# A decoder step on one core: the key/value stage rebuilt around pairs of tiles and four split slots

## The chip, the cores and the metric

The kernel runs on one core of a Trainium2 chip. The metric is the device time of one execution in microseconds. Three executions of the kernel before took 1482.45, 1484.24 and 1484.52 us; the median is 1484.24.

## What is computed

One inference step of a one-layer decoder, for a prompt of 1024 tokens and 8 sample tokens, model width 1024, all in float32. The outputs are the tokens, the caches, and for the prompt the keys and values of a memory of 256 tokens. What touches this change is the first half of it:

```python
def memory_kv(mem, g, w_k, w_v):          # mem: 256 tokens x 1024
    m = rms_norm(mem, g)
    return m @ w_k, m @ w_v               # keys and values, both are outputs

h = rms_norm(x, norm_mix_g)               # x: 1032 tokens x 1024
proj = h @ w_in                           # 2576 columns, 21 tiles of 128 with padding
...
x = x + token_mix(...)                    # convolution and gated linear attention, w_out
x = x + cross_attn(rms_norm(x), mk, mv)   # w_q, w_o
x = x + square(relu(rms_norm(x) @ w_up)) @ w_down
y = rms_norm(x, final_g)
```

## The kernel before

**Tiles.** Activations lie with features on the 128 partitions and the 1032 tokens (T) along the free side, in blocks of 344 (CB). Weights come as tiles of 1024 x 128 (512 KB, 8 slices k of 128 x 128), numbered t. Tiles 0 to 15 are w_xk and w_xv (stage "kv", T_IN = 16), then 21 tiles of w_in, and so on up to the last.

**Split products.** Each product is made in float32r as three: high x high, high x low, low x high. So each weight tile is split: ACT copies it, rounded, to the high half (w_high, L676), POOL subtracts that from the raw tile in two halves of four slices and gets the low half (lo, L602). PE then multiplies (tile_product, L1166, in the kv stage 8 slices x 3 products = 24 matmuls of 256 columns, m_op being the split memory). The raw tile comes by a DMA that SP issues (load_w, L453). In the kv stage there are four raw slots (w_raw, w_more; tile t in slot t % 4) but two split slots in w_split: w_high(t) waits until tile t-2 is multiplied (tile_done), and load_w(t) until lo(t-4) is done. An engine takes its own instructions in the order in which they are written.

**The kv stage.** m_raw (the memory) comes in two DMAs, par (gains) in one. ACT issues the four loads of x (load_x, L691), walpha and conv_cache in its own queue. ACT makes the eight high parts of memory (L705) with the gain in them, DVE the low ones (L1736). ACT squares the memory (L707), DVE adds the squares over the slices (L1744), PE sums them over the partitions with a matrix of ones (sums, L1185), behind tile 0, and ACT makes the root by Ln and Exp (L711, L713): m_rstd. DVE evacuates each tile from the bank set it lies in, PS[t % 2], with m_rstd as factor (kv_evac, L1760). Keys go out from m_out; values are transposed by PE in pairs (mv_turn, L1199), read by ACT (mv_read, L738), and go out. SP's stores of mk and mv stand in its order between the loads, with waits for kv_evac or mv_read ahead of them (L476, L479).

**The norm of x in the same stage.** ACT squares the eight parts of x (square_x, L718 and L722), DVE adds them into acc in SBUF (add_square, L1769), PE sums over the partitions behind tile 8, into the two small banks M (L1185, three products, the third of which waits for a bank), ACT makes 1/rms by Ln and Exp (norm, L683 and L687) into rstd in SBUF, DVE multiplies x by it and the gain (x_scale, L1772), ACT rounds to a_op high (x_high, L732), DVE subtracts (x_low, L1735). The first input tile (first_in_tile, L1281) waits for x_low(k) slice by slice and writes all three banks of PS[0]; the other input tiles (in_block, L1267) follow block by block. From the second input tile on DVE works on the convolution's taps (L1806), which accumulate in PS[1].

In the code ORDER, PLACE and SLOTS set what PE does between tiles; SP, POOL, ACT, PE and DVE each have a block of their own in build(). The three functions of the norm and the order of ACT's and DVE's work in the stage are written out by hand:

```python
for t in range(2, 11):                                   # ACT
    w_high(t, t % 2)
    for k in {3: (0, 1), 4: (2, 3), 6: (4, 5), 7: (6, 7)}.get(t, ()):
        square_x(k)
norm(1, 1)
...
for n_kv in range(9):                                    # DVE
    kv_evac(n_kv)
    for k in {2: (0, 1), 3: (2, 3), 5: (4, 5), 6: (6, 7)}.get(n_kv, ()):
        add_square(k)
```

## Time and profile before

| | us |
|---|---|
| median of three executions | 1484.24 |
| the profiled execution | 1484.24 |
| its span in the trace | 1482.2 |
| PE busy in the span | 1446.8 (98%) |
| DVE / ACT / POOL busy | 611.1 / 461.8 / 387.0 |
| first product of PE (kv stage) | 11.05 |
| first input tile | 87.49 |
| granted clock, mean of the span | 0.994 |

The page cuts the span into 40 slices of 37 us; a digit is the busy share in tenths:

```profile
PE   5799999999999999999999999999999999999998
PEld 5789999999899999979999999999999999999997
DVE  3659999998553355633321200121011111012114
ACT  5532243436733333413232200132012221022324
POOL 4754222111722211102222222222222222222220
PEclk9999999999999999999999999999999999999999
```

PE is TensorE's matmuls, PEld its weight loads, DVE VectorE, ACT ScalarE, POOL GpSimd; PEclk is the clock granted to TensorE, where 1.00 is 2.4 GHz and 0.50 is 1.2 GHz. Times in all rows are microseconds from the span's start unless marked ns.

### The profile page before, as it was taken

To read this page: it belongs to the slowest core of one execution; us is meant where nothing else is said; L and a number is where in the kernel's file an instruction comes from. 1 tells how busy PE (TensorE), PEld (TensorE's weight loads), DVE (VectorE), ACT (ScalarE), POOL (GpSimd) and SP (SyncE) were. 2 spreads that over 40 slices of the span, in tenths; PEclk is the share of its full clock that TensorE was granted. 3 is DMA by queue.
4 is the path that set the end of the run, shared out by engine and by line. 5 is a ranking of instruction groups with operands and counts; after the bars stand their busy time and mean duration, and the time that the engine had idled before them with its cause. 6 is when DMAs were issued, how large, how long until landed. Compare 5 with 4: busy or idle time off the path is not lost.

```text
span 1482.2 us, 22520 instructions
## 1 busy us (share of the span) xinstructions
PE 1446.8 (98%) x9501; PEld 1414.9 (95%) x9501; DVE 611.1 (41%) x693; ACT 461.8 (31%) x622; POOL 387.0 (26%) x298
## 2 busy tenths in 40 slices
PE   5799999999999999999999999999999999999998
PEld 5789999999899999979999999999999999999997
DVE  3659999998553355633321200121011111012114
ACT  5532243436733333413232200132012221022324
POOL 4754222111722211102222222222222222222220
PEclk9999999999999999999999999999999999999999
DMA  7421151102252511392111111111111111111113
GB/s 283 151 74 50 51 51 47 40 29 56 92 186 101 185 58 35 104 372 75 43 43 57 43 47 52 43 42 57 42 42 42 42 57 42 56 37 48 43 42 115
DMA packets 47357, 114.06 MB, mean 77 GB/s; under 512 B 7720, under 2 KB 23352, under 8 KB 45888
## 3 DMA queue, kind: packets, MB, share of 16 engines
q1 hardware_dynamic: 46544, 108.41, 23.7%
q10 hardware_dynamic: 752, 4.75, 0.8%
q8 instruction: 48, 0.79, 0.2%
q14 instruction: 13, 0.11, 0.0%
HBM read 100.85 MB, written 12.30 MB: 76 GB/s over the span
## 4 chain that ended last, share of the span: by engine, by line
PE 93%; DVE 4%; ACT 1%; POOL 1%; issue 1%; DMA 0%; ACTq 0%; SPq 0%; DVEq 0%
PE ps L1166 59%; PE ps L1267 14%; PE ps L1539 5%; PE m L1237 2%; PE ps L1573 2%; PE ps L1671 1%; PE ps L1492 1%; PE m L1452 1%; POOL w_split L602 1%; PE ps L1281 1%; DVE ps L1806 1%; PE ps L1552 1%; PE m L1367 1%; PE m L1516 1%; PE ps L1483 1%
## 5 line engine op out<-in xcount | busy, mean ns | idle before, releaser
L602 POOL TENSOR_TENSOR w_split<-w_raw,w_split 128x512 fp32r<-128x512 f32 x234 | 326.4, 1416 | 1044.7 <-ACT w_split L676 1044.5
L1166 PE MATMUL ps<-a_op,w_split 128*128 128x344 f32 x3168 | 499.4, 319 | 0.0
L1166 PEld LDWEIGHTS ps<-a_op,w_split 128*128 128x128 f32 x3168 | 497.8, 188 | 0.5 <-issue 0.5
L1166 PE MATMUL ps<-b_op,w_split 128*128 128x344 f32 x2304 | 362.6, 319 | 0.0
L1166 PEld LDWEIGHTS ps<-b_op,w_split 128*128 128x128 f32 x2304 | 361.7, 188 | 0.2
L1267 PE MATMUL ps<-a_op,w_split 128*128 128x344 f32 x1440 | 233.2, 321 | 0.0
L1267 PEld LDWEIGHTS ps<-a_op,w_split 128*128 128x128 f32 x1440 | 226.5, 188 | 1.7 <-issue 1.4
L676 ACT ACTIVATE w_split<-w_raw 128x1024 fp32r<-128x1024 f32 x117 | 122.9, 1051 | 258.5 <-PE ps L1166 252.4
L1806 DVE SCALAR_TENSOR_TENSOR ps<-conv_in,par,ps 128x1024 f32<-128x1024 f32 x116 | 149.7, 1291 | 3.6
L2192 DVE SCALAR_TENSOR_TENSOR tmp<-ps,rstd 128x1032 f32<-128x1032 f32 x32 | 39.5, 1233 | 215.1 <-PE ps L1166 203.2
L2202 DVE TENSOR_TENSOR x_res<-x_res,ps 128x1032 f32 x24 | 29.5, 1229 | 230.8 <-PE ps L1166 230.8
L1097 ACT ACTIVATE tmp<-tmp 128x1032 f32<-128x1032 f32 x32 | 34.1, 1067 | 259.1 <-DVE tmp L2192 259.1
L1539 PE MATMUL ps<-b_op,w_split 128*128 128x344 f32 x504 | 83.3, 322 | 0.0
L1539 PEld LDWEIGHTS ps<-b_op,w_split 128*128 128x128 f32 x504 | 79.8, 188 | 0.6
L2014 DVE TENSOR_TENSOR x_res<-x_res,ps 128x1032 f32<-128x1032 f32 x22 | 27.0, 1228 | 129.2 <-PE ps L1166 124.8
L1166 PE MATMUL ps<-m_op,w_split 128*128 128x256 f32 x384 | 57.9, 313 | 21.8 <-POOL w_split L602 21.8
L1166 PEld LDWEIGHTS ps<-m_op,w_split 128*128 128x128 f32 x384 | 54.3, 218 | 24.8 <-issue 17.8
L2197 DVE TENSOR_TENSOR a_op<-tmp,a_op 128x1032 f32 x32 | 39.5, 1234 | 80.8 <-ACT a_op L1100 80.8
L979 ACT ACTIVATE b_op<-x_res,par 128x1032 fp32r<-128x1032 f32 x16 | 18.6, 1160 | 101.9 <-DVE x_res L2014 101.9
L1100 ACT ACTIVATE a_op<-tmp 128x1032 f32 x32 | 34.2, 1067 | 4.3
L1736 DVE SCALAR_TENSOR_TENSOR b_op<-x_res,par,b_op 128x1032 fp32r<-128x1032 f32 x16 | 22.8, 1422 | 19.7 <-ACT b_op L979 19.7
L722 ACT ACTIVATE tmp<-x_res 128x1032 f32<-128x1032 f32 x19 | 20.1, 1056 | 33.1 <-DVE x_res L2014 33.0
(245 smaller groups left out, 1070.6 us busy)
## 6 DMA issues: line engine op xcount, KB each, us to landing
w_raw<-in_wt SPq DMA_DIRECT2D x117, 512.0 KB, 3.5
cache_b<-in_cache_v SPq DMA_DIRECT2D x8, 1024.0 KB, 12.2
x_in<-in_x ACTq DMA_DIRECT2D x4, 1032.0 KB, 10.7
x_spill<-x_res SPq DMA_DIRECT2D x8, 516.0 KB, 2.6
w_more<-in_wt SPq DMA_DIRECT2D x8, 512.0 KB, 4.1
cache_a<-in_cache_k SPq DMA_DIRECT2D x2, 2048.0 KB, 11.2
cache_b<-in_cache_k SPq DMA_DIRECT2D x2, 2048.0 KB, 11.8
x_res<-in_x SPq DMA_DIRECT2D x1, 3096.0 KB, 11.1
```

The lines of the kernel that those rows point to most:

```text
L602: gp.tensor_tensor(w_split[:, slot, 1, part, :], src, w_split[:, slot, 0, part, :].bitcast(F32), ALU.subtract).then_inc(w_low_done, 1)
L676: act.activation(w_split[:, slot, 0, :, :], src, ACT.Copy).then_inc(w_high_done, 1)
L1097: act.activation(tmp[:, j, :], tmp[:, j, :], ACT.Square).then_inc(scalar_step, 1)
L1100: act.activation(dst, tmp[:, j, :], ACT.Copy).then_inc(hidden_high, 1)
L1166: last = pe.matmul(ps[:, c0 // CB, 0:w], w_split[:, slot, wp, k, :], src[:, k, xp, c0:c0 + w], start=(k == 0 and j == 0), stop=(k == KT - ...
L1237: last = pe.matmul(bank[:, j * C:(j + 1) * C], k_t[:, pair, NS + C * c:NS + C * (c + 1)], qz[pair][:, C * c:C * (c + 1)], start=True, stop ...
L1267: last = pe.matmul(PS[0][:, b, 0:CB], w_split[:, p % 2, wp, k, :], a_op[:, k, xp, b * CB:(b + 1) * CB], start=(k == 0 and j == 0), stop=(k ...
L1539: last = pe.matmul(PS[0][:, b, 0:CB], w_split[:, t % 2, wp, k, :], b_op[:, k, xp, b * CB:(b + 1) * CB], start=(k == 0 and j == 0), stop=(k ...
L1573: last = pe.matmul(PS[m][:, b, 0:CB], w_split[:, t % 2, wp, k, :], a_op[:, k, xp, b * CB:(b + 1) * CB], start=(k == 0 and j == 0), stop=(k ...
L1806: link(dve.scalar_tensor_tensor(out=conv_acc, in0=src, scalar=t_, in1=conv_acc, op0=ALU.mult, op1=ALU.add))
L2192: dve.scalar_tensor_tensor(out=cols(tmp[:, j, :]), in0=pcols(bank_of(T_FF + j)), scalar=0.0, in1=cols(rstd[:, :]), op0=ALU.max, op1=ALU.mu ...
L2197: dve.tensor_tensor(dst, tmp[:, j, :], hi, ALU.subtract).then_inc(hidden_low, 1)
```

## The change

Four split slots: two more (w_split_more) lie in a_op's parts 6 and 7, which are not yet in use; kv tile t takes split slot t % 4, w_high(t) waits for tile t-4, and x_high(6), x_high(7) wait for tiles 14 and 15 to be done. Two kv tiles share one bank of PS[0], and three banks take turns (kv_pair); DVE evacuates a pair at once (128x512), so 8 evacuations stand for 16. PS[1] is free for x: the running sum of squares, the sums over the partitions and 1/rms lie there; only the last add goes to acc in SBUF. Memory's 1/rms is Sqrt on ACT and a reciprocal on DVE; a small Sqrt ahead of everything and a small Ln behind the root are new. The memory's sums stand behind tile 2. All loads go through SP's queue, par and w0 first, the parts of x behind tiles 3, 5, 6 and 7. The stores of mk and mv and the third pair of mv transposes change their place. ACT's and DVE's order is written anew.

```diff
 for _g in range(4):
-    SLOTS.setdefault((PLACE["kv", 9 + 2 * _g] + 1, LAST_BLOCK), []).append(("mv", _g))
+    SLOTS.setdefault((PLACE["kv", 9 + 2 * _g] + (1, 1, 2, 1)[_g], LAST_BLOCK), []).append(("mv", _g))
 for _j in range(2 * NB):
...
 assert o_sm + DC * 4 <= o1 + SPLIT + KT * T * 4
+w_split_more = [at(f"w_split_more{i}", (KT - 2 + i) * 2 * T * 4, [P, 2, KT, P], F32R) for i in range(2)]
 w_more = at("w_more", o_u, [P, 2, KT, P])
...
+def split(t, slot):
+    return w_split_more[slot] if isinstance(t, int) and t < T_IN and t % 4 >= 2 else w_split[:, slot]
+def kv_pair(g):
+    return PS[0][:, g % NB, :].rearrange("p (a n) -> p a n", a=2)
 a_products = tmp[:, :, :].rearrange("p a n -> p (a n)")
...
 def _(sp):
-    sp.dma_start(m_raw[:, 0:4, :], a["mem"][:, 0:4, :]).then_inc(m_part[0], 16)
     sp.dma_start(par[:, :], a["par"]).then_inc(params_loaded, 16)
...
+    def load_x(i):
+        sp.dma_start(x_in[:, 2 * i:2 * i + 2, :], a["x"][:, 2 * i:2 * i + 2, :]).then_inc(x_part[i], 16)
     load_w(0, 0, False)
-    sp.dma_start(m_raw[:, 4:8, :], a["mem"][:, 4:8, :]).then_inc(m_part[1], 16)
+    for i in range(2):
+        sp.dma_start(m_raw[:, 4 * i:4 * i + 4, :], a["mem"][:, 4 * i:4 * i + 4, :]).then_inc(m_part[i], 16)
     for t in range(1, 4):
         load_w(t, t % 2, False)
+    load_x(0)
     for t in range(4, T_XO + 3):
         load_w(t, t % 2)
+        if 5 <= t < 8:
+            load_x(t - 4)
+        if t == 9:
+            sp.dma_start(walpha[:, :], a["w_alpha"]).then_inc(w_alpha_loaded, 16)
+            sp.dma_start(conv_smp[:, :, :, :], a["conv_cache"]).then_inc(conv_cache_loaded, 16)
         for q in range(4):
-            if t == PLACE["kv", 2 * q + 1] + 5:
+            if t == 2 * q + 8:
                 sp.wait_ge(ps_free, PLACE["kv", 2 * q + 1] + 1)
                 sp.dma_start(o["mk"][:, 2 * q:2 * q + 2, :], m_out[:, q % 2, :, :]).then_inc(mem_kv_stored[q % 2], 16)
-            if t == PLACE["kv", 9 + 2 * q] + (6, 6, 7, 7)[q]:
+            if t == (16, 17, 19, 20)[q]:
                 wait_read(sp, ("mv", q))
...
             src = raw(t)[:, part, :] if isinstance(t, int) else w_raw[:, slot, part, :]
-            gp.tensor_tensor(w_split[:, slot, 1, part, :], src,
-                             w_split[:, slot, 0, part, :].bitcast(F32), ALU.subtract).then_inc(w_low_done, 1)
+            gp.tensor_tensor(split(t, slot)[:, 1, part, :], src,
+                             split(t, slot)[:, 0, part, :].bitcast(F32), ALU.subtract).then_inc(w_low_done, 1)
...
             act.wait_ge(w_loaded[slot], (count - 4) * 16 + 16)
-        if not isinstance(t, int) or t >= 2:
-            act.wait_ge(tile_done, t - 1)
+        if not isinstance(t, int) or t >= 4:
+            act.wait_ge(tile_done, t - 3 if isinstance(t, int) and t < T_IN + 2 else t - 1)
         src = raw(t) if isinstance(t, int) else w_raw[:, slot, :, :]
-        act.activation(w_split[:, slot, 0, :, :], src, ACT.Copy).then_inc(w_high_done, 1)
+        act.activation(split(t, slot)[:, 0, :, :], src, ACT.Copy).then_inc(w_high_done, 1)
...
-    def load_x(i):
-        act.dma_start(x_in[:, 2 * i:2 * i + 2, :], a["x"][:, 2 * i:2 * i + 2, :]).then_inc(x_part[i], 16)
+    act.wait_ge(eps_ready, 1)
+    act.activation(small[:, 129:130], small[:, 128:129], ACT.Sqrt)
+    w_high(0, 0)
     act.wait_ge(params_loaded, 16)
-    load_x(0)
     for k in range(KT):
...
             act.wait_ge(m_part[k // 4], 16)
-        if k == 4:
-            w_high(0, 0)
-            for i in range(1, 4):
-                load_x(i)
-            act.dma_start(walpha[:, :], a["w_alpha"]).then_inc(w_alpha_loaded, 16)
-            act.dma_start(conv_smp[:, :, :, :], a["conv_cache"]).then_inc(conv_cache_loaded, 16)
         act.activation(m_op[:, k, 0, :], m_raw[:, k, :], ACT.Copy,
                        scale=par[:, G_MEM + k:G_MEM + k + 1]).then_inc(operand_high, 1)
+    w_high(1, 1)
+    w_high(2, 0)
     act.activation(msq[:, :, :], m_raw[:, :, :], ACT.Square).then_inc(square_done, 1)
-    w_high(1, 1)
-    act.wait_ge(eps_ready, 1)
-    act.wait_ge(sums_ready, 1)
-    act.activation(m_rstd[:, :], M[0][:, 0:MEM], ACT.Ln, bias=small[:, 128:129], scale=1.0 / D).then_inc(sums_read, 1)
-    act.wait_ge(sums_read, 1)
-    act.activation(m_rstd[:, :], m_rstd[:, :], ACT.Exp, scale=-0.5).then_inc(rstd_ready, 1)
+    w_high(3, 1)
+    def mem_root():
+        act.wait_ge(sums_ready, 1)
+        act.activation(m_rstd[:, :], M[0][:, 0:MEM], ACT.Sqrt, bias=small[:, 128:129], scale=1.0 / D).then_inc(sums_read, 1)
+        act.activation(small[:, 131:132], small[:, 128:129], ACT.Ln)
...
             act.wait_ge(x_part[k // 2], 16)
-        square(x_in[:, k, :], None, k, 1)
+        if k == 0:
+            act.activation(pcols(1), cols(x_in[:, 0, :]), ACT.Square).then_inc(square_done, 1)
+        else:
+            square(x_in[:, k, :], None, k, 1)
+    def norm_x():
+        act.wait_ge(sums_ready, 1 + NB)
+        act.activation(cols(rstd[:, :]), pcols(1), ACT.Ln, bias=small[:, 128:129], scale=1.0 / D).then_inc(sums_read, NB)
+        act.wait_ge(sums_read, 1 + NB)
+        act.activation(pcols(1), cols(rstd[:, :]), ACT.Exp, scale=-0.5).then_inc(rstd_ready, 1)
...
         act.wait_ge(x_normed, k + 1)
+        if k >= KT - 2:
+            act.wait_ge(tile_done, T_IN - KT + 1 + k)
         act.activation(a_op[:, k, 0, :], x_in[:, k, :], ACT.Copy).then_inc(operand_high, 1)
...
-    for t in range(2, 11):
+    square_x(0)
+    square_x(1)
+    w_high(4, 0)
+    w_high(5, 1)
+    mem_root()
+    square_x(2)
+    square_x(3)
+    w_high(6, 0)
+    square_x(4)
+    square_x(5)
+    w_high(7, 1)
+    square_x(6)
+    w_high(8, 0)
+    square_x(7)
+    for t in range(9, 13):
         w_high(t, t % 2)
-        for k in {3: (0, 1), 4: (2, 3), 6: (4, 5), 7: (6, 7)}.get(t, ()):
-            square_x(k)
-    norm(1, 1)
-    for k in range(KT):
-        x_high(k)
-        if k >= 1:
-            w_high(10 + k, k % 2)
-        if k in (2, 4, 6):
-            mv_read((k - 2) // 2)
+    norm_x()
+    w_high(13, 1)
+    x_high(0)
+    x_high(1)
+    w_high(14, 0)
+    x_high(2)
+    x_high(3)
+    mv_read(0)
+    w_high(15, 1)
+    x_high(4)
+    x_high(5)
+    w_high(16, 0)
+    mv_read(1)
+    w_high(17, 1)
+    x_high(6)
+    x_high(7)
+    mv_read(2)
...
+    def kv_product(n):
+        if n % 2 == 0 and n >= 2 * NB:
+            pe.wait_ge(ps_free, n - 2 * NB + 2)
+        bank = kv_pair(n // 2)[:, n % 2, :]
+        w_ = split(n, n % 2)
+        for k in range(KT):
+            if k % (KT // 2) == 0:
+                pe.wait_ge(w_low_done, n * 2 + 1 + k // (KT // 2))
+            if n == 0:
+                pe.wait_ge(operand_low, k + 1)
+            for j, (wp, xp) in enumerate(((0, 0), (0, 1), (1, 0))):
+                last = pe.matmul(bank, w_[:, wp, k, :], m_op[:, k, xp, :], start=(n % 2 == 0 and k == 0 and j == 0),
+                                 stop=(n % 2 == 1 and k == KT - 1 and j == 2))
+        last.then_inc(tile_done, 1)
+    def x_sums():
+        pe.wait_ge(squares_summed, 1 + KT)
+        for b in range(NB):
+            pe.matmul(PS[1][:, b, 0:CB], ones[:, :], acc[:, b * CB:(b + 1) * CB], start=True, stop=True).then_inc(sums_ready, 1)
     def first_in_tile():
...
-        pe.wait_ge(ps_free, T_IN - 1)
+        pe.wait_ge(ps_free, T_IN)
         for k in range(KT):
...
                 if name[1] == 0:
-                    pe.wait_ge(sums_read, 4)
+                    pe.wait_ge(sums_read, 1)
                 mv_turn(name[1])
...
     for n_kv in range(T_IN):
-        tile_product(n_kv, n_kv % 2, m_op, [(0, MEM)], wait_lo(0) if n_kv == 0 else no_wait)
-        if n_kv == 0:
+        kv_product(n_kv)
+        if n_kv == 2:
             sums(1, 0, MEM)
         if n_kv == 8:
-            sums(9, 1)
+            x_sums()
         between(n_kv, LAST_BLOCK)
...
-    def kv_evac(n):
-        p = PLACE["kv", n]
-        dve.wait_ge(tile_done, p + 1)
-        if n == 0:
+    def kv_evac(g):
+        dve.wait_ge(tile_done, 2 * g + 2)
+        if g == 0:
             dve.wait_ge(rstd_ready, 1)
-        g = n // 2
-        if n < 8:
-            dst = m_out[:, g % 2, n % 2, :]
-            if g >= 2 and n % 2 == 0:
+        if g < 4:
+            dst = m_out[:, g % 2, :, :]
+            if g >= 2:
                 dve.wait_ge(mem_kv_stored[g % 2], 16)
         else:
-            dst = mvt[:, g % 2, n % 2, :]
-            if g >= 6 and n % 2 == 0:
+            dst = mvt[:, g % 2, :, :]
+            if g >= 6:
                 wait_full(dve, ("mv", g - 6))
-        dve.tensor_tensor(dst, PS[p % 2][:, 0, 0:MEM], m_rstd[:, :], ALU.mult).then_inc(ps_free, 1)
+        dve.tensor_tensor(dst, kv_pair(g), m_rstd[:, :].unsqueeze(1).broadcast_to([P, 2, MEM]), ALU.mult).then_inc(ps_free, 2)
...
             dve.engine_nop().then_inc(squares_summed, 1)
-        else:
-            dve.wait_ge(squares_summed, 1 + k)
-            dve.tensor_tensor(acc[:, :], acc[:, :], tmp[:, k % 2, :], ALU.add).then_inc(squares_summed, 1)
+            return
+        dve.wait_ge(squares_summed, 1 + k)
+        if k == KT - 1:
+            dve.wait_ge(sums_ready, 1)
+        dst = pcols(1) if k < KT - 1 else cols(acc[:, :])
+        dve.tensor_tensor(dst, pcols(1), cols(tmp[:, k % 2, :]), ALU.add).then_inc(squares_summed, 1)
...
     def x_scale(k):
-        dve.scalar_tensor_tensor(out=x_in[:, k, :], in0=x_in[:, k, :], scalar=par[:, G_MIX + k:G_MIX + k + 1],
-                                 in1=rstd[:, :], op0=ALU.mult, op1=ALU.mult).then_inc(x_normed, 1)
+        dve.scalar_tensor_tensor(out=cols(x_in[:, k, :]), in0=cols(x_in[:, k, :]), scalar=par[:, G_MIX + k:G_MIX + k + 1],
+                                 in1=pcols(1), op0=ALU.mult, op1=ALU.mult).then_inc(x_normed, 1)
...
-    for n_kv in range(9):
-        kv_evac(n_kv)
-        for k in {2: (0, 1), 3: (2, 3), 5: (4, 5), 6: (6, 7)}.get(n_kv, ()):
-            add_square(k)
+    add_square(0)
+    add_square(1)
+    dve.wait_ge(sums_read, 1)
+    dve.reciprocal(m_rstd[:, :], m_rstd[:, :]).then_inc(rstd_ready, 1)
+    add_square(2)
+    kv_evac(0)
+    add_square(3)
+    kv_evac(1)
+    add_square(4)
+    add_square(5)
+    kv_evac(2)
+    add_square(6)
+    add_square(7)
+    kv_evac(3)
     dve.wait_ge(rstd_ready, 2)
...
     x_scale(1)
-    for k in range(7):
-        kv_evac(9 + k)
+    kv_evac(4)
+    x_scale(2)
+    x_scale(3)
+    x_scale(4)
+    kv_evac(5)
+    x_scale(5)
+    x_scale(6)
+    x_scale(7)
+    kv_evac(6)
+    for k in range(4):
         x_low(k)
-        if k + 2 < KT:
-            x_scale(k + 2)
-    x_low(KT - 1)
+    kv_evac(7)
+    for k in range(4, KT):
+        x_low(k)
+    dve.wait_ge(x_normed, KT)
     n_taps = 0
     conv_acc = PS[1][:, 0:2, :]
...
```

## Rows read from the trace of the kernel before

**Rows 1.** Windows: stretch, length, busy us (instructions) per engine, clock, DMA share, GB/s.
```profile
99.47:340.00 240.53, 240.53 (x1576) 237.26 (x1576) 220.47 (x200) 83.93 (x134) 63.53 (x63) 1.00 0.22 47
```

**Rows 2.** Timeline of PE: start, length, instructions, [idle before, releaser].
```profile
11.05 5.46 PE L1166 MATMUL ps<-m_op,w_split 128*128 128x256 f32 x24 [11.05 <-POOL w_split L602]
...
24.94 11.64 PE L1166 MATMUL ps<-m_op,w_split 128*128 128x256 f32 x72 [3.17 <-POOL w_split L602]
...
52.15 1.32 PE L1185 MATMUL m<-acc,ones 128*128 128x344 f32 x4
55.38 0.84 PE L1185 MATMUL m<-acc,ones 128*128 128x344 f32 x2 [1.91 <-ACT rstd L683]
55.80 6.05 PE L1166 MATMUL ps<-m_op,w_split 128*128 128x256 f32 x48
...
65.68 8.67 PE L1166 MATMUL ps<-m_op,w_split 128*128 128x256 f32 x48 [2.85 <-POOL w_split L602]
74.19 0.60 PE L1199 MATMUL m<-ident,mvt 128*128 128x128 f32 x4
...
87.49 11.54 PE L1281 MATMUL ps<-a_op,w_split 128*128 128x344 f32 x72 [0.61 <-issue]
```

**Rows 3.** Timeline of DVE in the key/value stage.
```profile
14.44 3.72 DVE L1744 TENSOR_REDUCE acc<-msq 128x256 f32<-128x2048 f32 x1 [0.78 <-ACT msq L707]
...
30.43 0.42 DVE L1760 TENSOR_TENSOR m_out<-ps,m_rstd 128x256 f32<-128x256 f32 x1 [7.07 <-PE ps L1166]
```

**Rows 4.** Windows again, two short ones; the clock is the third number from the end.
```profile
26.00:28.00 2.00, 2.00 (x11) 2.00 (x11) 0.00 (x0) 0.30 (x1) 2.00 (x3) 0.50 0.70 49
38.00:40.00 2.00, 1.52 (x13) 1.31 (x12) 0.29 (x1) 1.64 (x2) 2.00 (x2) 1.00 0.43 168
```

**Rows 5.** Waits from 0 to 120: us in total, times, longest.
```profile
POOL w_split L602 <- ACT w_split L676: 50.3, 15, 8.9
PE ps L1166 <- POOL w_split L602: 21.8, 13, 11.1
```

**Rows 6.** Timeline of ACT.
```profile
8.55 1.06 ACT L676 ACTIVATE w_split<-w_raw 128x1024 fp32r<-128x1024 f32 x1 [0.20 <-DMA m_raw<-in_mem]
...
20.79 1.28 ACT L713 ACT_TABLE_LOAD   x1
22.08 0.42 ACT L713 ACTIVATE m_rstd<-m_rstd 128x256 f32<-128x256 f32 x1
```

**Rows 7.** Timeline of POOL.
```profile
9.69 2.51 POOL L602 TENSOR_TENSOR w_split<-w_raw,w_split 128x512 fp32r<-128x512 f32 x2 [7.88 <-ACT w_split L676]
```

**Rows 8.** DMA issues at 2.1 to 2.5: size, us from issue to landing.
```profile
m_raw<-in_mem SPq DMA_DIRECT2D x1, 512.0 KB, 6.3
```

**Rows 9.** Windows again, for the last column, GB/s.
```profile
3.00:8.00 5.00, 0.00 (x0) 0.00 (x0) 0.82 (x3) 2.64 (x5) 0.00 (x0) 1.00 0.95 330
9.00:24.00 15.00, 9.01 (x50) 8.49 (x50) 6.70 (x7) 10.02 (x13) 5.49 (x5) 1.00 1.02 419
...
7.00:8.00 1.00, 0.00 (x0) 0.00 (x0) 0.82 (x3) 1.00 (x4) 0.00 (x0) 1.00 0.83 266
```

**Rows 10.** Timeline of ACT at the kernel's end, behind the Sqrt of L1150.
```profile
1464.19 0.51 ACT L1139 ACTIVATE tmp<-x_res 128x384 f32<-128x384 f32 x1
...
1468.85 0.26 ACT L1145 ACTIVATE small<-m,small 128x3 f32<-128x3 f32 x1 [0.93 <-PE m L1700]
```

**Rows 11.** DVE's instructions by line: ns least/median/most, first and last start.
```profile
L1806 DVE SCALAR_TENSOR_TENSOR ps<-conv_in,par,ps x116: 1207/1290/1356, 117.7 to 334.0; 128x1024 f32<-128x1024 f32 x116
...
L1772 DVE SCALAR_TENSOR_TENSOR x_in<-x_in,par,rstd x8: 1289/2314/2348, 59.2 to 86.1; 128x1032 f32<-128x1032 f32 x8
...
L1735 DVE TENSOR_TENSOR a_op<-x_in,a_op x8: 1222/1979/2328, 62.0 to 90.7; 128x1032 fp32r<-128x1032 f32 x8
```

**Rows 12.** DVE's groups by shape, 95 to 600: busy us, mean ns.
```profile
L2077 DVE TENSOR_TENSOR a_op<-ps,a_op 128x512 fp32r<-128x512 f32 x8 | 5.3, 688 | 5.7 <-ACT a_op L1038 5.7
```

**Rows 13.** ACT's groups by shape: busy us, mean ns.
```profile
L917 ACT ACTIVATE ps<-rstd 128x1032 f32<-128x1032 f32 x1 | 1.0, 1036 | 0.0
```

More of the change, by code:

```diff
@@ L1784, in _ @@
             x_scale(1)
-            for k in range(7):
-                kv_evac(9 + k)
+            kv_evac(4)
[8 more added lines that the diff above has]
+            for k in range(4):
                 x_low(k)
-                if k + 2 < KT:
-                    x_scale(k + 2)
-            x_low(KT - 1)
+            kv_evac(7)
+            for k in range(4, KT):
+                x_low(k)
+            dve.wait_ge(x_normed, KT)
             n_taps = 0
+            conv_acc =            n_taps = 0
             conv_acc = PS[1][:, 0:2, :]
```

## The prediction

> **What bounds the kernel now.** The span is 1482.2 us and the execution took 1484.24, so 2.0 us lie outside it; 1484.24 is also the median of the three runs, and the sum is made against it. I read the windows first: in the input projection PE is busy in all of 240.5 us, at granted clock 1.00, with products of 344 columns one behind the other; nothing is to be won there [rows 1]. The slices of the page show PE below nine tenths only in the first three, where the key/value stage lies. So the change is worth what it takes out of the stretch from PE's first product (11.05) to the first input tile (87.49), 76.4 us [rows 2].
>
> How long must that stretch be? 48 products, which are two tiles, took 6.05 us without a gap: 3.03 us per tile [rows 2], 48.5 for sixteen. The other 28 us are seen in the timeline: a first tile of 5.46 us, a gap of 3.17 before 24.94, one of 2.85 before 65.68, and small ones [rows 2]. The tile begun at 24.94 was evacuated at 30.43 [rows 3]: 5.5 us, slow again. At 26 to 28 us the granted clock is 0.50, which is 1.2 GHz; at 38 to 40 it is 1.00 although PE had just stood still for 0.5 us [rows 4], and a gap of 1.91 before 55.38 was followed by tiles of 3.03 [rows 2]. So here gaps of up to 1.9 us cost themselves, and gaps of 2.85 and more cost a slow tile as well, 2.4 us.
>
> Who makes the gaps? The table of waits: PE waited 21.8 us in 13 times for POOL's low halves of the weights, and POOL 50.3 us for ACT's high halves [rows 5], and ACT in its turn for PE to give a slot of w_split back: a ring of two slots with all of ACT's other work inside it. No link is slow by itself: ACT's half takes 1.06 us [rows 6], POOL's two 2.51 [rows 7], against PE's 3.03.
>
> **Part by part** (times in us from the span's start).
>
> Start. The second part of memory landed 6.3 us after 2.21, at 8.5 [rows 8]; up to it the queue carries 1.66 MB. At 330 GB/s [rows 9] w0, now second in the queue with 0.61 MB up to its end, lands 3.2 earlier, at 5.3, and the first part of memory (1.14 MB) at 6.9. ACT's high half of w0 is there at 6.4, POOL's first low half at 7.6. Memory's first high and low parts take 0.45 and 0.5, and up to 0.5 more beside POOL. PE starts at 8.5 in place of 11.05. The first tile stays slow, 5.46 [rows 2]: 14.0. With half a us more at the low clock the second ends at 17.3.
>
> Four slots. w_high(t) now waits for tile t-4 instead of t-2. ACT: w_high 1 and 2 end at 11.4 and 12.7, memory's square (1.9) at 14.6, w_high 3 at 15.7, two squares of x and w_high 4 and 5 at 19.7 and 20.8. POOL, at 2.51 a tile, is done with tiles 1, 2, 3 at 13.9, 16.4, 18.9 and with 4, 5 at 22.2, 24.7. PE wants them at 14.0, 17.3, 21.0, 24.0, 27.0. PE's waits for weights go; what hides POOL's work is a lead of 1 to 2.3 us, and where that is used up each further us is one of PE's.
>
> Memory's norm. The reduce takes 3.72 [rows 3] and ends by 18.4; its product now stands behind tile 2 (20.3) and costs PE 0.6. Ln and Exp with a table load each become one Sqrt. Its load is moved ahead of the first data, where ACT was idle, and at the end of the kernel Square and Sqrt follow each other without a load [rows 10]. A load of Ln's table is added behind it. The reciprocal of 128x256 has no row. Bounds: 0.42, the other DVE operation of that size, and 3.72, the longest of the stage [rows 3]. I take 1, as it is one input and 256 columns; either end lies beside PE's work, since DVE's next square (x part 1) comes at 21 to 24.
>
> Squares of x. Seven adds with an operand in PSUM, 1.3 each by their nearest row, L1806 [rows 11]; the last, behind x part 3, ends at 34 to 37, and PE asks for it at the end of tile 8, 39.2. The evacuations, 16 of 0.42 [rows 3], become 8 of 128x512 at 0.69 [rows 12]: 5.5 us for 6.7, hidden by three banks.
>
> Loads. The issues of x, walpha and conv_cache leave ACT, which gains a us or so in idle time. But 4.2 MB of x now share one FIFO with the weights, and w8 is 10.1 MB deep. SP alone moved 330 GB/s at 3 to 8 us, with ACT's queue beside it 419 at 9 to 24 [rows 9]. From 8.5 on, w8 lands at 34.0 by the one and at 28 by the other; tile 8 wants it at 33.7. So at the lower rate it holds to 0.3. SP's new waits hold up w9 (behind evacuation 0, about 26), w10, w11 and w17 (behind the first read of mv, about 52), all wanted 4 us or more after they land.
>
> PE's stretch. Tile 2 ends at 20.3, the sums at 20.9, tile 8 at 39.15. The three sums of x cost 1.9 (two took 1.32 [rows 2]): 41.05; tiles 9 and 10: 47.1. Here is a new wait: the transpose of mv pair 0 wants evacuation 4, which DVE makes behind x_scale 0 and 1. The chain from 41.15: Ln 1.1, load of Exp's table 1.28 [rows 6], Exp into PSUM 1.04 [rows 13], two x_scale of 1.29 [rows 11], evacuation 0.69: 47.9 with the handovers. PE waits 0.8. Then transposes (0.45, they overlap the next tile [rows 2]), tiles 11 and 12, transposes, tile 13: 57.9; tiles 14 and 15: 64.0; transposes 64.4. A second new wait: the first input tile wants all banks of set 0, hence evacuation 7, behind evacuation 6 (58.6) and four x_low. Those have both inputs in SBUF, 1.22 us at the least and 1.98 in the median beside POOL [rows 11]. POOL splits tile 17 from 59.1 to 62.6, so they end at 64.9 and evacuation 7 at 65.6. PE's gap there is 1.2, against 0.6 before. The first input tile starts at 65.65 instead of 87.49: **21.8 us less**, 1462.4. Its last four x_low are due one per 1.44 us, with four in hand. What follows shifts as a whole: DVE ends its x_low as late behind PE's start as before, and its 220 of 240 us [rows 1] begin with the second input tile.
>
> **One rule weighed.** ACT's rows show a table load at 20.79 of 1.28 us and its Exp at 22.08, at once behind it [rows 6]. The Trainium skill (ScalarE: Activation LUTs, What ACT_TABLE_LOAD costs) adds some 1380 ns of drain to the 1283 ns of a load. By it evacuation 4 and all behind it would come 1.4 us later, 1463.8. The trace differs, and the sum goes by the trace.
>
> **Rivals.** (a) DVE goes on colliding with POOL. Before, x_scale, both tensor inputs in SBUF, took 2.31 in the median against 1.29 at the least. The change moves one input to PSUM; L1806, with one there, took 1.21 to 1.36 in all of 116 times [rows 11], with POOL busy 63.5 us of that stage [rows 1]: against the rival. If it holds, evacuation 4 comes at 50.1, evacuation 5 at 57.8, 1.2 late for its transposes, evacuation 7 near 71.4: 5.8 us more, 1468.2. The Trainium skill (SBUF — State Buffer, Who interferes with whom) says that a DVE operation with at most one SBUF input doesn't contend with GpSimd; by that rule (a) falls, and the trace agrees.
>
> (b) Data come late. At the lowest us seen, 266 GB/s [rows 9], w8 lands at 41.4 and tile 8 starts at 43.8, 7.7 late: 1470.1, and 2.4 more if PE's gap comes in one piece.
>
> (c) The ring is now POOL's. At 3.5 a tile, as with DVE beside it, ten tiles cost 0.5 each more than PE's own time: 1467.4.
>
> (d) No gain: ACT's order takes back what the slots give, as w_high stands in one in-order engine behind squares that wait for adds and for x. 22 us need two gaps of 3, two slow tiles, and 1 us at each other tile; the leads above would have to go at every tile, and no row has ACT that far behind.
>
> (e) Slower: the queue of (b), further. At 21.8 late w8 lands at 55.5, which is 10.1 MB in 52 us; from 193 GB/s down the change loses, at 180 w8 lands at 59.5 and the time is 1488. The lowest row is 266.
>
> **How the numbers follow.** Forecast 0.70, with 1460 (start at 8.0, no new wait of PE) and 1465 as its ends; (a) 0.07, (b) 0.08, (c) 0.07, (d) 0.04, (e) 0.04. The range 1459.8 to 1470 takes in the forecast, (a), (c) and half of (b), and leaves the rest. About 0.2%, 3 us, can be told from no change. Faster: forecast with (a), (b), (c), 0.92; same (d), 0.04; slower (e), 0.04.
>
> **What would show it.** In the profile of the changed kernel: the first product at 8.5; no granted clock of 0.50 behind 16 us; PE's waits for POOL under 3 us; adds and x_scale at 1.3; gaps of about 1 us ahead of the first transposes and of the first input tile, which starts at 66; 1394.7 us from there to the end, as before. It is wrong if w6 to w8 land behind 26, 30 and 34, if PE has a gap over 2 us, or if a table load stands between memory's square and its root.

## The result, and the profile after

Four executions of the changed kernel took 1463.53 us in the median (1462.52 to 1465.59), four of the kernel before 1484.38 (1482.45 to 1484.70). The ratio is 0.9864, with a 95% interval of 0.9847 to 0.9881: 20.9 us less, where 21.8 were forecast. The profiled execution took 1464.26 us with a span of 1462.5. In the table the kernel before is the execution of its profile, 1484.24.

| | before | forecast | after |
|---|---|---|---|
| first product | 11.05 | 8.5 | 8.16 |
| first input tile | 87.49 | 65.65 | 67.67 |
| from there to the end | 1394.7 | 1394.7 | 1394.8 |
| execution time, after: median | 1484.24 | 1462.4 | 1463.53 |

So all of the gain lies where it was looked for (19.8 us between the two profiles), and nothing behind the first input tile gave or took any. PE's timeline in the key/value stage, to be held against [rows 2] (start, length, instruction, in brackets the idle time before it and who ended it):

```profile
8.16 0.98 PE L1331 MATMUL ps<-m_op,w_split 128*128 128x256 f32 x3 [8.16 <-DVE m_op L1805]
9.50 6.89 PE L1331 MATMUL ps<-m_op,w_split 128*128 128x256 f32 x45 [0.35 <-DVE m_op L1805]
16.23 2.96 PE L1331 MATMUL ps<-m_op,w_split_more 128*128 128x256 f32 x24
...
22.30 5.86 PE L1331 MATMUL ps<-m_op,w_split 128*128 128x256 f32 x48
28.00 5.80 PE L1331 MATMUL ps<-m_op,w_split_more 128*128 128x256 f32 x48
...
36.48 1.90 PE L1339 MATMUL ps<-acc,ones 128*128 128x344 f32 x6
...
41.03 2.96 PE L1331 MATMUL ps<-m_op,w_split_more 128*128 128x256 f32 x24
47.40 1.09 PE L1246 MATMUL m<-ident,mvt 128*128 128x128 f32 x4 [3.40 <-DVE mvt L1828]
48.14 5.21 PE L1331 MATMUL ps<-m_op,w_split_more 128*128 128x256 f32 x24
...
67.67 11.59 PE L1350 MATMUL ps<-a_op,w_split 128*128 128x344 f32 x72 [2.13 <-DVE mvt L1828]
```

Three things are to be seen. From 8.16 to 44.0 PE has no gap but 0.35 us, where before it had five up to there, two of them over 1.7; POOL is named nowhere as the one that PE waited for [rows 5]. Two rows of two tiles each start 5.70 us apart (22.30, 28.00), so a tile costs 2.85. And two gaps are left, both ended by DVE's evacuation of a pair of value tiles: 3.40 ahead of the first transposes, and 2.13 ahead of the first input tile. The tile behind the first of them took 5.21.

### The profile page after: what moved, and what is told of

It is laid out like the page before. It is cut to its first block, busy times and chain, and to the rows that moved or that the text cites. A ratio compares the mean times of both kernels' runs of the same rounds, so it can differ in the third digit from the quotient of the medians.

```text
span 1462.5 us, 22505 instructions
## 1 busy us (share of the span) xinstructions
PE 1439.4 (98%) x9501; PEld 1410.3 (96%) x9501; DVE 602.1 (41%) x686; ACT 458.3 (31%) x619; POOL 377.4 (26%) x298
## 3 DMA queue, kind: packets, MB, share of 16 engines
q1 hardware_dynamic: 47296, 113.17, 24.5%
## 4 chain that ended last, share of the span: by engine, by line
PE 95%; DVE 3%; DMA 1%; ACT 1%; issue 0%; POOL 0%; SPq 0%; DVEq 0%; ACTq 0%
PE ps L1213 59%; PE ps L1314 14%; PE ps L1608 5%; PE ps L1331 2%; PE m L1284 2%; PE ps L1642 2%; PE ps L1740 1%; PE ps L1561 1%; PE m L1521 1%; PE ps L1350 1%; DVE ps L1896 1%; PE ps L1621 1%; PE m L1436 1%; PE m L1585 1%; PE ps L1552 1%; PE m L1534 1%
## 5 line engine op out<-in xcount | busy, mean ns | idle before, releaser
L620 POOL TENSOR_TENSOR w_split<-w_raw,w_split 128x512 fp32r<-128x512 f32 x234 | 321.5, 1395 | 1044.9 <-ACT w_split L694 1044.8
L1331 PE MATMUL ps<-m_op,w_split 128*128 128x256 f32 x192 | 26.0, 294 | 8.5 <-DVE m_op L1805 8.5
L1331 PEld LDWEIGHTS ps<-m_op,w_split 128*128 128x128 f32 x192 | 24.7, 199 | 9.1 <-issue 8.1
## 6 DMA issues: line engine op xcount, KB each, us to landing
cache_a<-in_cache_k SPq DMA_DIRECT2D x2, 2048.0 KB, 11.1
```

Of the source, the lines that this page charges most:

```text
L620: gp.tensor_tensor(split(t, slot)[:, 1, part, :], src, split(t, slot)[:, 0, part, :].bitcast(F32), ALU.subtract).then_inc(w_low_done, 1)
L1331: last = pe.matmul(bank, w_[:, wp, k, :], m_op[:, k, xp, :], start=(n % 2 == 0 and k == 0 and j == 0), stop=(n % 2 == 1 and k == KT - 1 an ...
```

## The experiments

The kernel before was run again in each group, with medians of 1483.18, 1483.01 and 1482.93. So the last column goes by the ratios: (ratio - 0.9864) x 1483, how much slower than the changed kernel. The intervals are some 2.5 us to each side. Two such ratios enter each difference, so that differences under 3.5 us or so are read from the traces, not from the times. The pairing of the evacuations and the new order of ACT's and DVE's work were never undone by themselves; what each of them is worth is not shown. In the edits below the semaphore calls are left out of some lines, and "..." stands for lines left out.

| kernel | median | ratio to before (95%) | us against changed |
|---|---|---|---|
| e1 two split slots | 1476.05 | 0.9950 (0.9934 to 0.9967) | +12.8 |
| e3 x in SBUF | 1472.70 | 0.9931 (0.9915 to 0.9948) | +9.9 |
| e7 two queues | 1468.53 | 0.9904 (0.9888 to 0.9921) | +5.9 |
| e8 sums behind tile 0 | 1467.70 | 0.9895 (0.9878 to 0.9911) | +4.6 |
| e4 Ln and Exp | 1466.87 | 0.9890 (0.9873 to 0.9906) | +3.9 |
| e2 transposes later | 1464.05 | 0.9864 (0.9845 to 0.9884) | 0.0 |
| e10 evacuation 7 sooner | 1461.34 | 0.9857 (0.9840 to 0.9873) | -1.0 |
| e5 both of these (e2 and e10) | 1457.40 | 0.9827 (0.9810 to 0.9843) | -5.5 |
| e6 both, norm of x sooner | 1456.66 | 0.9821 (0.9805 to 0.9837) | -6.4 |
| e9 four slots alone | 1481.90 | 0.9990 (0.9980 to 1.0000) | (-1.5 against before) |

**Parts undone or alone.** First the slots.

```diff
 def split(t, slot):
-    return w_split_more[slot] if isinstance(t, int) and t < T_IN and t % 4 >= 2 else w_split[:, slot]
+    return w_split[:, slot]
...
-        if not isinstance(t, int) or t >= 4:
-            act.wait_ge(tile_done, t - 3 if isinstance(t, int) and t < T_IN + 2 else t - 1)
+        if not isinstance(t, int) or t >= 2:
+            act.wait_ge(tile_done, t - 1)
```

> The changed kernel with two split slots again (w_high waits for tile t-2), all else as changed. My theory, that the slots took PE's waits for weights away (before: 21.8 us and two slow tiles): PE waits for POOL again at most tiles, 8 to 14 us more than the changed kernel, about 1474 us, since pairs, banks and the shorter norm of memory keep their part. Rival, that the new order of ACT and the loads did it and the slots little: under 3 us more, below 1467.

12.8 us slower, as the theory had it, but not by the way it named. PE's timeline and ACT's of this kernel:

```profile
56.52 1.09 PE L1246 MATMUL m<-ident,mvt 128*128 128x128 f32 x4 [7.78 <-DVE mvt L1828]
...
45.96 1.06 ACT L694 ACTIVATE w_split<-w_more 128x1024 fp32r<-128x1024 f32 x1 [3.56 <-PE ps L1331]
48.84 1.06 ACT L694 ACTIVATE w_split<-w_raw 128x1024 fp32r<-128x1024 f32 x1 [1.82 <-PE ps L1331]
49.80 1.10 ACT L749 ACTIVATE rstd<-ps,small 128x1032 f32<-128x1032 f32 x1
```

PE waits little for weights (2.5 us in three times); it waits 7.78 us at the first transposes, since 1/rms of x comes 9.1 us later than in the changed kernel. Half of that, 4.6, is there when PE's sums of x are done (43.0 for 38.4). The other 4.5 arise behind them: ACT stands 3.56 and 1.82 us for PE to free a slot, and the norm of x is next in its order. So half of that delay is what stands behind the wait in ACT's order.

The other way round, the slots alone in the kernel before (split() and the wait as in the change, x_high(6) and x_high(7) behind tiles 14 and 15):

```diff
-                if not isinstance(t, int) or t >= 2:
-                    act.wait_ge(tile_done, t - 1)
+                if not isinstance(t, int) or t >= 4:
+                    act.wait_ge(tile_done, t - 3 if isinstance(t, int) and t < T_IN + 2 else t - 1)
```

> The kernel before with four split slots and nothing else of the change (w_high waits for tile t-4, x_high 6 and 7 for tiles 14 and 15). My theory, that slots and the order of ACT's work need each other: w_high(2) still stands behind memory's root by Ln and Exp, so the first gap of 3 us and its slow tile stay, and w_high(10) on stand behind the norm and x_high; what goes are ACT's waits for PE (13.1 us) and with them the small gaps: 6 to 9 us faster than the kernel before, 1475. Rival, that the slots are nearly the whole change: 15 us faster or more. Rival, that alone they give nothing, as order and data bind: under 3 us.

The theory missed: 1.5 us, at the edge of the interval; the third reading was right. ACT's waits for PE to give a slot back are gone, but PE waits for POOL as long as before, 24.5 us (15.3 and 9.2 by slot) against 21.8 [rows 5]. POOL's timeline, and two rows of DVE's, show why:

```profile
62.02 3.92 POOL L607 TENSOR_TENSOR w_split_more<-w_more,w_split_more 128x512 fp32r<-128x512 f32 x2 [6.46 <-ACT w_split_more L681]
65.90 9.00 POOL L607 TENSOR_TENSOR w_split<-w_raw,w_split 128x512 fp32r<-128x512 f32 x4
...
68.05 1.22 DVE L1742 TENSOR_TENSOR a_op<-x_in,a_op 128x1032 fp32r<-128x1032 f32 x1
69.19 2.32 DVE L1779 SCALAR_TENSOR_TENSOR x_in<-x_in,par,rstd 128x1032 f32<-128x1032 f32 x1
```

POOL first stands idle for 6.46 us: w_high(11) is behind the norm of x and x_high(1) in ACT's old order. From then on it works without a pause and needs 4.5 us per tile in place of 2.51 [rows 7], with x_scale and x_low, both inputs in SBUF, beside it. The first gap of 3.2 us stays too (PE resumes at 25.70, behind memory's root by Ln and Exp). So the slots alone meet two other limits, the order of ACT's work and POOL's pace. Which of the two weighs more here is not shown: no run has the slots with only one of them lifted. The next kernel leaves x in SBUF with all else as changed, and it still keeps 10 us of the gain (0.9931).

```diff
-    act.activation(pcols(1), cols(x_in[:, 0, :]), ACT.Square)        # square_x(0)
+    act.activation(rstd[:, :], x_in[:, 0, :], ACT.Square)
-    dst = pcols(1) if k < KT - 1 else cols(acc[:, :])                # add_square
-    dve.tensor_tensor(dst, pcols(1), cols(tmp[:, k % 2, :]), ALU.add)
+    dst = rstd[:, :] if k < KT - 1 else acc[:, :]
+    dve.tensor_tensor(dst, rstd[:, :], tmp[:, k % 2, :], ALU.add)
-    act.activation(pcols(1), cols(rstd[:, :]), ACT.Exp, scale=-0.5)  # norm_x; x_scale reads rstd
+    act.activation(rstd[:, :], rstd[:, :], ACT.Exp, scale=-0.5)
```

> The changed kernel with the running sum of x's squares and 1/rms of x in SBUF (rstd) again, so that the adds and x_scale have both inputs in SBUF; all waits and orders as changed. My theory, that DVE and POOL collide only then: the adds go from 1.24 to about 2 us, x_scale from 1.28 to 1.9 to 2.3 in the median, POOL's halves beside them from 1.27 to 1.75; evacuation 4 comes 1.5 to 2 us later and evacuation 7 2 to 6 later: 3 to 6 us slower than the changed kernel, 1468. Rival, that they are hidden in DVE's waits: within 1 us.

DVE's instructions by line (ns least/median/most), here and, second, in the changed kernel, and PE's timeline here:

```profile
L1839 DVE TENSOR_TENSOR rstd<-rstd,tmp x6: 1609/1908/2290, 17.9 to 32.1; 128x1032 f32<-128x1032 f32 x6
L1842 DVE SCALAR_TENSOR_TENSOR x_in<-x_in,par,rstd x8: 1280/2305/2350, 47.9 to 62.3; 128x1032 f32<-128x1032 f32 x8
...
30.45 1.68 PE L1331 MATMUL ps<-m_op,w_split_more 128*128 128x256 f32 x12 [0.51 <-POOL w_split_more L620]
52.31 1.09 PE L1246 MATMUL m<-ident,mvt 128*128 128x128 f32 x4 [4.61 <-DVE mvt L1828]
74.17 12.89 PE L1350 MATMUL ps<-a_op,w_split 128*128 128x344 f32 x72 [4.21 <-DVE mvt L1828]
```

```profile
L1839 DVE TENSOR_TENSOR ps<-ps,tmp x6: 1231/1242/1242, 17.9 to 32.3; 128x1032 f32<-128x1032 f32 x6
L1842 DVE SCALAR_TENSOR_TENSOR x_in<-x_in,par,ps x8: 1281/1284/1290, 44.2 to 56.5; 128x1032 f32<-128x1032 f32 x8
```

The mechanism is the expected one, and DVE's durations are; POOL's halves took up to 2.25 us where 1.75 was expected, and the whole cost 9.9 us (7.8 by the spans) where 3 to 6 were expected. POOL's slower halves put gaps of 0.4 to 0.6 us into tiles 6 to 8. They also free the raw slots later: SP issues w12 at 38.4 instead of 34.7, ACT waits 4.06 us for it, and Ln behind it begins 3.8 us later, at 44.43. With that evacuation 4 is 4.9 us late where 1.5 to 2 were expected. Both gaps at DVE's evacuations grow to over 4 us, and both are followed by slow products.

Memory's norm by Ln and Exp (DVE's reciprocal goes with it):

```diff
-    act.activation(small[:, 129:130], small[:, 128:129], ACT.Sqrt)   # at the start
...
-    act.activation(m_rstd[:, :], M[0][:, 0:MEM], ACT.Sqrt, bias=small[:, 128:129], scale=1.0 / D)
-    act.activation(small[:, 131:132], small[:, 128:129], ACT.Ln)
+    act.activation(m_rstd[:, :], M[0][:, 0:MEM], ACT.Ln, bias=small[:, 128:129], scale=1.0 / D)
+    act.wait_ge(sums_read, 1)
+    act.activation(m_rstd[:, :], m_rstd[:, :], ACT.Exp, scale=-0.5)
```

> The changed kernel with memory's 1/rms by Ln and Exp (two table loads, no reciprocal, no small Sqrt and Ln). My theory: the root itself ends 1.5 us later, at 23.1, which ACT's waits for x and w_high's for data (2.2 us and 2.8) hide; Ln for x then needs a table load of its own, 1.28 us in the chain to evacuation 4: 1.3 us slower, 1464.8. Rival, that the early delay hits PE's weights: 3 us and more.

3.9 us by the ratio; by the spans 2.2 (1464.7 against 1462.5). Two things show in ACT's timeline. The expected one is the load for x ahead of Ln. The other, at the start, I had left out: without the small Sqrt the first table load comes when w0 has landed, and what is behind it is late.

```profile
5.25 1.28 ACT L694 ACT_TABLE_LOAD   x1 [5.25 <-DMA w_raw<-in_wt]
...
41.69 1.28 ACT L749 ACT_TABLE_LOAD   x1
42.98 1.12 ACT L749 ACTIVATE rstd<-ps,small 128x1032 f32<-128x1032 f32 x1
```

PE's first product is at 9.38 instead of 8.16, and PE is 2.2 us late from tile 2 on. But PE stands 3.53 us at the first transposes here as well, so what counts there is Ln, at 42.98 instead of 40.67: 2.3 us late, of which the load is 1.28 and w_high(12), 0.9 later than in the changed kernel, most of the rest. So the expected 1.3 us is there; what the small Sqrt at the start is worth by itself no run shows.

Memory's sums behind tile 0 (n_kv == 0 in place of n_kv == 2):

> The changed kernel with the memory's sums behind tile 0 again in place of behind tile 2. DVE's reduce ends at 17.8, tile 0 at 13. My theory: PE stands 4.5 to 5 us there, and as that is over 2.85 the next tile is slow by 2.4 us; all behind it shifts, and only ACT's waits for data in the stage give 1 to 2 us back: 4 to 7 us slower, 1469. Rival, that the chain to evacuation 4 hides it, as it starts from the squares of x and not from PE's tiles: under 2 us slower.

4.6 us, within the range, with a gap of 3.21 instead of 4.5:

```profile
17.93 1.21 PE L1232 MATMUL m<-acc,ones 128*128 128x256 f32 x2 [3.21 <-DVE acc L1813]
18.57 4.46 PE L1331 MATMUL ps<-m_op,w_split 128*128 128x256 f32 x24
...
51.44 0.63 PE L1246 MATMUL m<-ident,mvt 128*128 128x128 f32 x4 [1.22 <-DVE mvt L1828]
...
69.29 13.07 PE L1350 MATMUL ps<-a_op,w_split 128*128 128x344 f32 x72 [2.12 <-DVE mvt L1828]
```

What was lost at the start was given back in part at the first transposes (a gap of 1.22 for 3.40). By the spans the kernel is 3.1 us slower: 1.6 by the start of the first input tile and 1.5 by its slow products (13.07 for 11.59), which the theory did not have.

The loads of x, walpha and conv_cache from ACT's queue again (in short: each call stands for its dma_start, which leaves SP's block):

```diff
     act.wait_ge(params_loaded, 16)
+    load_x(0)                                   # issued by ACT
     for k in range(KT): ...                     # memory's high parts
+    load_x(1); load_x(2); load_x(3); walpha; conv_smp
     w_high(1, 1)
```

> The changed kernel with the loads of x, walpha and conv_cache issued by ACT again, in its own queue: x part 0 ahead of the memory's high parts, the others behind them. My theory, that one queue costs little and the order saves ACT's issuing: ACT issues for 0.45 us before PE's first product and for 2.2 us ahead of w_high(1), so PE starts 0.5 later and waits 1 to 2 us for tile 1; w10 to w12 land sooner, and the chain to evacuation 4 starts 1 to 2 us sooner, which gives part of it back: within 2 us of the changed kernel, 1464.5. Rival, that the queue with 330 to 390 GB/s holds the stage up: 3 us faster.

5.9 us slower (5.0 by the medians, 3.1 by the spans), outside what either reading gave. ACT's timeline:

```profile
12.79 1.06 ACT L685 ACTIVATE w_split_more<-w_more 128x1024 fp32r<-128x1024 f32 x1 [1.24 <-DMA w_more<-in_wt]
...
24.10 1.06 ACT L685 ACTIVATE w_split<-w_raw 128x1024 fp32r<-128x1024 f32 x1 [2.71 <-DMA w_raw<-in_wt]
```

The issuing is the small part (w_high(1) starts at 10.5, not 9.9). In a queue of their own the parts of x share the transfer with the weights: w2 to w5 land late, memory's root, which stands behind w_high(5), comes at 25.1 for 19.7, and PE waits 0.35 and 1.70 for tiles 5 and 6. w10 to w12 did not land sooner, as the theory had it: ACT waits 4.9 us for them in place of 3.7, and Ln begins at 44.81. The single queue is worth its order, weights ahead of what is wanted later. It is no matter of its rate: from 9 to 24 us the two queues moved 420 GB/s and the one 392, and the kernel with two was the slower.

**What is left in the changed kernel.** The two gaps, each by itself and together.

```diff
-    SLOTS.setdefault((PLACE["kv", 9 + 2 * _g] + (1, 1, 2, 1)[_g], LAST_BLOCK), []).append(("mv", _g))
+    SLOTS.setdefault((PLACE["kv", 9 + 2 * _g] + (3, 2, 2, 1)[_g], LAST_BLOCK), []).append(("mv", _g))
```

> The changed kernel with the transposes of mv pairs 0 and 1 behind tiles 12 and 13 in place of 10 and 12. In the changed kernel PE stands 3.4 us for evacuation 4 ahead of them, and the next tile takes 5.2 us at the low clock in place of 2.9. My theory, that DVE's chain behind 1/rms of x is the bound: PE reaches the end of tile 15 some 5.6 us sooner, at 59.3, but DVE's order holds evacuation 7 until 63; the first input tile starts at 63 to 64 instead of 67.7, and as PE's gap is now 3 to 4 us there, that tile runs slow for 5 us and gives 2.5 back: 1.5 to 2.5 us faster than the changed kernel, 1461.5. Rival, that a gap costs only itself: 4 to 4.5 us faster. Rival, that DVE's last x_low sets the end whatever PE does: no difference.

The gap did move, and PE was through tile 15 at 59.9; then it stood 4.92 us and the input tile took 13.10 in place of 11.59:

```profile
65.39 13.10 PE L1350 MATMUL ps<-a_op,w_split 128*128 128x344 f32 x72 [4.92 <-DVE mvt L1828]
...
56.10 8.64 DVE L1804 TENSOR_TENSOR a_op<-x_in,a_op 128x1032 fp32r<-128x1032 f32 x4
```

The median moved by 0.5 us and the spans differ by 0.8; the interval, 2.9 us to each side, holds no difference and the expected 1.5 to 2.5. The input tile started at 65.39, later than the expected 63 to 64, because the four x_low now lay wholly beside POOL: 8.64 us for 6.86. So DVE's order looked like the bound, and the next kernels change it:

```diff
-    for k in range(4):
+    for k in range(2):
         x_low(k)
     kv_evac(7)
-    for k in range(4, KT):
+    for k in range(2, KT):
         x_low(k)
```

> The changed kernel with evacuation 7 behind two x_low in place of four, transposes where the change has them. My theory: the gap of 3.4 us and the slow tile ahead of tile 11 stay, and only the second gap (2.1 us before the first input tile) shrinks, to 0.8: 1.3 to 1.9 us faster than the changed kernel, 1462. Rival, that both gaps hang together (DVE's work only moves): no difference.

> The kernel with the transposes two tiles later, and in DVE's order evacuation 7 behind two x_low in place of four. My theory, that in the kernel before this one the gap had only moved to the first input tile (4.9 us, behind four x_low of 2.1 beside POOL) and a slow tile with it: evacuation 7 comes about 61, PE's gap ahead of the first input tile is 1 to 1.5 us, and the tile runs at full clock: 11.5 us, started at 61.5 in place of 67.7; 5.5 to 6.5 us faster than the changed kernel, 1457.5. Rival, that x_low as a whole bounds the tile, since eight must be made ahead of its end whatever the order: PE would then wait inside the first input tile, which would take 14 us or more, and the kernel would gain under 3 us.

Alone it gave 1.0 by the ratio, 2.2 by the medians; its interval holds the 1.3 to 1.9 expected, but no difference as well. With the transposes moved it gave 5.5 (medians: 1457.40, expected 1457.5). By the ratios the two changes give 0 and 1 apart and 5.5 together. In e2 the first gap only moved to the input tile; e10 shortens the second gap (0.40 in its profile) and can do nothing for the first, which lies ahead of the place that it changes. PE's timeline of e5, then that of e10:

```profile
60.80 11.57 PE L1350 MATMUL ps<-a_op,w_split 128*128 128x344 f32 x72 [0.62 <-DVE mvt L1828]
```

```profile
46.63 0.63 PE L1246 MATMUL m<-ident,mvt 128*128 128x128 f32 x4 [1.57 <-DVE mvt L1828]
...
62.72 11.59 PE L1350 MATMUL ps<-a_op,w_split 128*128 128x344 f32 x72 [0.40 <-DVE mvt L1828]
```

Up to the first transposes e10 and the changed kernel are the same program, and yet the gap there is 1.57 in the one profile and 3.40, with a slow tile, in the other. The traces show the two parts of the difference: in e10 the first two tiles took 9.25 us in place of 8.07, so that PE came 1.06 later, and evacuation 4 came 0.77 sooner. The profile of e10 is the fastest of its four executions, so the 5.0 us between the two spans is not what the change is worth. Four executions of the changed kernel lie within 3.1 us, of e10 within 3.6, of e2 within 4.6, but of e5 and e6, which have no gap over 0.7 behind the first product, within 0.5 and 0.4. A gap alone does not explain it, though: e1 and e4, with gaps of 7.78 and 3.53 us, lie within 0.4 and 0.9.

Last, on top of e5, ACT's norm of x ahead of w_high(12):

```diff
-    for t in range(9, 13):
+    for t in range(9, 12):
         w_high(t, t % 2)
     norm_x()
+    w_high(12, 0)
```

> As the one before, and ACT's norm of x ahead of w_high(12). In the changed kernel PE's sums of x were done at 38.3, but ACT began Ln at 40.7, behind w_high 10 to 12, which waited 3.7 us for their loads. My theory, that this wait for data sits in the chain: 1/rms comes 1.5 to 2 us sooner, and as PE's gap behind tile 15 is then nearly closed, 0.5 to 1.2 us come out of it: 1456.5. Rival: PE needs tile 12's weights, now later, and waits for them: no gain, or 1 us lost.

Ln started at 39.02 instead of 41.08 in e5 (40.67 in the changed kernel), so 1/rms came 2.0 us sooner as expected, PE did not wait for tile 12, and the gap ahead of the input tile went from 0.62 to 0.40. The two medians differ by 0.7 us, as expected, but the spans by 0.4 and the starts of the input tile by 0.3. All are less than the intervals tell apart, though no execution of e6 (1456.52 to 1456.95) took as long as any of e5 (1457.25 to 1457.74). It is the fastest kernel of this study: 1456.66, 1.8% under the kernel before.

## Why the prediction was right, and where its steps were off

**Right for the reasons given.** PE's waits for weights went, with their slow tiles (of the 21.8 us of [rows 5] the longest, 11.1, is the wait for the first product, so 10.7 were to be had between tiles); the stage behind shifted as a whole; the adds and x_scale took 1.24 and 1.28 with POOL beside them, so rival (a) fell, and e3 shows it was real: it would have cost more (9.9, by the spans 7.8) than the 5.8 I gave it. The evacuation (0.69) and the chain from Ln on (1.11, load 1.28, Exp 1.04) came as taken. The reciprocal, bounded by 0.42 and 3.72 and taken as 1, took 1.75, hidden as said:

```profile
20.17 1.75 DVE L1851 RECIPROCAL m_rstd<-m_rstd 128x256 f32<-128x256 f32 x1 [1.04 <-ACT m_rstd L725]
...
41.80 1.28 ACT L751 ACT_TABLE_LOAD   x1
43.09 1.04 ACT L751 ACTIVATE ps<-rstd 128x1032 f32<-128x1032 f32 x1
```

The load ends at 43.08 and Exp starts at 43.09: no drain of 1.4 us here either. The prediction gave 1463.8 us by the Trainium skill (ScalarE: Activation LUTs, What ACT_TABLE_LOAD costs); that lies near the measured time for another reason, the gaps below.

**Off: PE's time per tile.** I divided 6.05 us by two, but a row's length has the end of the last product in it. Start to start a tile takes 2.85, not 3.03. With the first two tiles 0.7 shorter than forecast as well, PE was through tile 8 at 36.5, not 39.15. Up to the first transposes the faster PE gained nothing by it, as the next points show. That the first two tiles were shorter was luck of this execution: in the profiles of the same start they took 8.0 to 9.3 us. Nor does the trace show the low clock that the forecast named for them: the granted clock at 10 to 12 reads 1.00, with 12 products in 2 us where 20 are made at 14 to 16. What slows them is not shown.

```profile
10.00:12.00 2.00, 2.00 (x12) 2.00 (x11) 2.00 (x5) 2.00 (x4) 0.97 (x1) 1.00 1.06 436
```

**Off: the loads.** The prediction said that w9 to w11, behind SP's new waits, are "all wanted 4 us or more after they land". Three rows of ACT's timeline say otherwise:

```profile
35.87 1.06 ACT L694 ACTIVATE w_split_more<-w_more 128x1024 fp32r<-128x1024 f32 x1 [1.95 <-DMA w_more<-in_wt]
37.78 1.06 ACT L694 ACTIVATE w_split_more<-w_more 128x1024 fp32r<-128x1024 f32 x1 [0.85 <-DMA w_more<-in_wt]
39.71 1.06 ACT L694 ACTIVATE w_split<-w_raw 128x1024 fp32r<-128x1024 f32 x1 [0.87 <-DMA w_raw<-in_wt]
40.67 1.11 ACT L749 ACTIVATE rstd<-ps,small 128x1032 f32<-128x1032 f32 x1
```

These are w10, w11 and w12. ACT waited 3.7 us for them, and Ln, behind them in its order, began 2.3 us after the sums were done (38.4). PE never wanted those weights so early; ACT did. I had asked when PE needs them, and not who stands behind the wait on ACT. e6 removes part of it. Nor was it SP's new waits that held them up, as SP's timeline shows:

```profile
27.17 0.33 SPq L461 DMA_DIRECT2D w_more<-in_wt  x1
...
30.84 0.33 SPq L461 DMA_DIRECT2D w_more<-in_wt  x1
34.68 0.33 SPq L461 DMA_DIRECT2D w_raw<-in_wt  x1
```

Each of the three goes out within 0.1 us of the end of POOL's low half of tile 6, 7 or 8 (27.15, 30.81, 34.6), which frees its raw slot, and lands 8.7, 6.9 and 5.0 us later. The ring of four raw slots set when they could start, and the prediction had no term for it.

**Off: the gaps.** Both errors meet at the first transposes. PE came 3.1 us sooner than forecast (44.0 for 47.1), evacuation 4 only 0.6 sooner (47.3 for 47.9): a gap of 3.40 where 0.8 was forecast, and by the forecast's own rule of 2.85 a slow tile, 2.2 us start to start. At the input tile x_low took 6.86 for 6.3, and the gap was 2.13 for 1.2. The forecast named both places and their releasers rightly and sized both too small. By its own signs of being wrong it failed in this: it allowed no gap over 2 us and no clock of 0.50 behind 16 us, and there are two such gaps, and a clock of 0.50 from 48 to 52. The sum up to the first input tile: the transposes 0.5 early, tile 11 slow by 2.0 against the forecast's 3.03, tiles 12 to 15 shorter by 0.7, the transposes 0.2 longer, x_low and the gap behind tile 15 another 1.1. That is 2.0 us late (67.67 for 65.65). The median came out only 1.1 off because the profiled execution is 0.7 slower than it and has 0.3 less outside its span. The spread of four executions is 3.1, so the closeness is partly luck.

**The rivals.** (b) and (c) didn't come about: w8 landed 9.4 us after its issue at 21.56, so at 31.0, between the 28 and 34 given; POOL, at 2.5 us a tile, was ahead of PE. It was close: POOL's first half of tile 8 was done at 33.4 and PE began the tile at 33.63. (c), POOL as the bound, is what e3 shows at tiles 6 to 8 and e9 behind 62 us, each with the slots and with x in SBUF. (d), slots given and nothing gained, is what e9 shows for the slots alone; it was priced at 0.04 as the fate of the full change. With x in SBUF the full change still gains 10 us (e3), so it is not PSUM alone that kept (d) off. (e) had no trace of it.

## What to carry to other kernels

In a stage where each engine takes its work in a fixed order, price a ring's slots by what stands behind the wait in that engine's order, and don't read a part's worth from one side: four slots gave 1.5 us alone and cost 12.8 when taken out of the whole, and the five parts undone here cost 37 us together, of a gain of 20.9. Where a gap is closed, write down the next wait on the same chain before counting the gain, since here the changes for two gaps gave 0 and 1 us alone, and 5.5 together. And put an operand of DVE's wide operations in PSUM when POOL works on the same stretch: of the five parts undone here it cost the second most.
